# A two-layer hybrid decoder step: the first section behind a norm multiplies rows that are not yet divided by their root mean square

## The reference

```python
def rms_norm(x, g):
    y = x * rsqrt(mean(x * x, axis=-1) + EPS)
    return y * g

for l in (0, 1):
    xn = rms_norm(h, norm_mix_g[l])
    z = xn @ w_in[l]                 # forget, query, value, v, u, ... by columns
    ...                              # gMLP branch, HGRN2 branch, two gates
    h = h + merged @ w_out[l]
    hn = rms_norm(h, norm_ffn_g[l])
    if l == 0:
        h = h + (silu(hn @ w_gate) * (hn @ w_up)) @ w_down
    else:
        h = h + moe_swiglu(hn, ...)  # top 2 of 8 experts
y = rms_norm(h, final_norm_g)
```

## Time and profile before

| | |
|---|---|
| median of three runs | 1613.34 us |
| profiled execution | 1615.19 us, of which span 1613.3 us |
| TensorE busy | 1578.9 us, 98% |
| VectorE, ScalarE busy | 1169.3 us, 1007.7 us |
| up to 800 us (both mixers, dense channel mixer) | 125 to 147 GB/s moved |
| from 800 us (experts) | 354 GB/s moved |

### The profile page before, as it was taken

How to read it: one execution, slowest core, us unless ns; L and a number is a source line. 1 busy time by engine, 2 the same in 40 slices (tenths; PEclk the granted TensorE clock), 3 DMA queues, 4 the chain that set the end, 5 groups by cost and what they waited for, 6 DMA issues and landing times.

```text
span 1613.3 us, 25617 instructions
## 1 busy us (share of the span) xinstructions
PE 1578.9 (98%) x8952; PEld 1403.4 (87%) x8953; DVE 1169.3 (72%) x1493; ACT 1007.7 (62%) x1192; POOL 98.7 (6%) x104
## 2 busy tenths in 40 slices
PE   8999999999999999999999999999999999999997
PEld 8889999999999978999988888888888888888785
DVE  6567437644444577734758989898998989899797
ACT  5663324434333576333467888888888887887785
POOL 3001110000000000021010001000100100000000
PEclk9999989999999999999999999999999999999999
DMA  7434444455445433433469999999999999999995
GB/s 240 132 106 135 149 136 127 130 145 154 140 144 159 126 114 109 131 138 131 127 203 363 375 374 375 368 379 362 381 378 377 376 371 382 364 372 369 373 366 200
DMA packets 223103, 398.57 MB, mean 247 GB/s; under 512 B 12369, under 2 KB 103553, under 8 KB 223025
## 3 DMA queue, kind: packets, MB, share of 16 engines
q1 hardware_dynamic: 215920, 372.84, 66.3%
q0 software_dynamic: 6752, 24.02, 4.9%
q10 hardware_dynamic: 352, 0.66, 0.1%
HBM read 383.84 MB, written 13.63 MB: 246 GB/s over the span
## 4 chain that ended last, share of the span: by engine, by line
PE 83%; DVE 6%; ACT 5%; issue 3%; DMA 3%; ACTq 0%; DVEq 0%; POOL 0%; SPq 0%; POOLq 0%
PE bank L1562 10%; PE bank L1564 10%; PE bank L1563 10%; PE bank L1907 10%; PE bank L1909 9%; PE bank L1908 9%; PE bank L1896 4%; PE bank L1898 4%; PE bank L1897 4%; ACT weights_high L709 2%; DMA weights_raw<-in_moe_w_up 1%; PE bank L1748 1%; PE bank L1874 1%; PE bank L1798 1%; PE bank L1793 1%
## 5 line engine op out<-in xcount | busy, mean ns | idle before, releaser
L1430 DVE TENSOR_TENSOR weights_low<-weights_raw,weights_high 128x1024 fp32r<-128x1024 f32 x522 | 619.4, 1222 | 77.9 <-ACT weights_high L940 68.4
L940 ACT ACTIVATE weights_high<-weights_raw 128x1024 fp32r<-128x1024 f32 x522 | 548.6, 1060 | 138.5 <-DMA weights_raw<-in_moe_w_up 46.0
L1026 DVE TENSOR_TENSOR weights_low<-weights_raw,weights_high 128x1024 fp32r<-128x1024 f32 (+1 forms) x186 | 224.6, 1213 | 294.7 <-ACT weights_high L709 294.5
L709 ACT ACTIVATE weights_high<-weights_raw 128x1024 fp32r<-128x1024 f32 (+1 forms) x186 | 193.6, 1045 | 246.8 <-PE bank L1564 236.2
L1562 PE MATMUL bank<-moving_high,weights_high 128*128 128x320 f32 x944 | 301.0, 319 | 0.7 <-DVE moving_low L1100 0.7
L1563 PE MATMUL bank<-moving_low,weights_high 128*128 128x320 f32 x944 | 296.9, 315 | 0.0
L1564 PE MATMUL bank<-moving_high,weights_low 128*128 128x320 f32 x944 | 296.9, 314 | 0.0
L1907 PE MATMUL bank<-weights_high,expert_in_high 128*128 128x512 f32 (+1 forms) x768 | 290.1, 378 | 2.6 <-DVE weights_low L1430 2.2
L1909 PE MATMUL bank<-weights_high,expert_in_low 128*128 128x512 f32 (+1 forms) x768 | 286.2, 373 | 0.0
L1908 PE MATMUL bank<-weights_low,expert_in_high 128*128 128x512 f32 (+1 forms) x768 | 286.1, 373 | 0.0
L1562 PEld LDWEIGHTS bank<-moving_high,weights_high 128*128 128x128 f32 x944 | 182.5, 193 | 4.0 <-DVE moving_low L1100 1.6
(11 more groups left out here) (327 smaller groups left out, 1837.6 us busy)
## 6 DMA issues: line engine op xcount, KB each, us to landing
weights_raw<-in_moe_w_gate SPq DMA_DIRECT2D x176, 512.0 KB, 5.5
weights_raw<-in_moe_w_up SPq DMA_DIRECT2D x176, 512.0 KB, 5.7
weights_raw<-in_moe_w_down SPq DMA_DIRECT2D x176, 512.0 KB, 5.3
weights_raw<-in_w_in SPq DMA_DIRECT2D x80, 512.0 KB, 3.6
weights_raw<-in_dense_w_gate SPq DMA_DIRECT2D x22, 512.0 KB, 3.7
weights_raw<-in_dense_w_up SPq DMA_DIRECT2D x22, 512.0 KB, 3.7
weights_raw<-in_w_out SPq DMA_DIRECT2D x16, 512.0 KB, 3.4
weights_raw<-in_dense_w_down SPq DMA_DIRECT2D x16, 512.0 KB, 3.4
```

Source lines behind the costliest of these rows:

```text
L709: fn(whi[:, p % RING, 0:n], raw[:, p % RING, 0:n], ACT.Copy).then_inc(high_done, 1)
L940: fn(whi[:, p % RING, 0:n], raw[:, p % RING, 0:n], ACT.Copy).then_inc(high_done, 1)
L1430: v.tensor_tensor(wlo[:, p % RING, 0:n], raw[:, p % RING, 0:n], whi[:, p % RING, 0:n].bitcast(F), ALU.subtract).then_inc(low_done, 1)
```

## The change

Behind each of the three norms the first section (forget 0, gate 0, forget 0 of layer 1) no longer waits for the norm. VectorE multiplies each group of the residual by the gain alone (`scale_residual`) as soon as the group is final, ScalarE makes the high part, VectorE the low part, and `products_as_scaled` multiplies them. TensorE takes the mean square behind the fifth of eight groups and spreads the inverse root behind the seventh. The second section uses the fully normed rows as before. ScalarE copies the first section's two output tiles out, and VectorE multiplies them by the inverse root (`first_outputs_divided`); for the gate the SiLU follows behind that. The identity turns inside the norms are gone (the 38 at the start stay).

```diff
+        def scale_residual(n, j):
+            col = (P_FFN if n % 2 else P_MIX) + KD * (n // 2) + j
+            v.tensor_scalar(xn[:, j, :], h[:, j, :], prm[:, col:col + 1], None, ALU.mult).then_inc(scaled_ready, 1)
+
+        def scaled_low_part(n, j):
+            high, low = scaled_operands(n)
+            dve.wait_ge(scaled_high, KD * n + j + 1)
+            v.tensor_tensor(low[:, j, :], xn[:, j, :], high[:, j, :].bitcast(F), ALU.subtract).then_inc(scaled_low, 1)
+
+        def first_outputs_divided(out, L, sec):
+            for j in (0, 1):
+                dve.wait_ge(act_emptied, tile[(L, sec, j)][3])
+                v.tensor_tensor(out[:, j, :], out[:, j, :], bank[4][:, 0:T], ALU.mult).then_inc(scaled_out, 1)
...
-        split_low(0, 0)
         dve.wait_ge(prm_ready, 1)
...
-        norm(0, after_inverse=lambda: split_low(0, 1))
+        scale_residual(0, 0)
+        split_low(0, 0)
+        for j in range(1, KD + 1):
+            if j < KD:
+                scale_residual(0, j)
+            if j == KD // 2:
+                split_low(0, 1)
+            scaled_low_part(0, j - 1)
+        norm(0, after_inverse=lambda: split_low(1, 0), midway=lambda: split_low(1, 1))
         v.tensor_tensor(lbt[:, 0], ...).then_inc(lb_ready, 1)
-        for c in range(1, AHEAD):
+        for c in range(2, AHEAD):
             split_low(c, 0)
             split_low(c, 1)
...
+        def products_as_scaled(L, sec, c, tiles, n):
...
+                    pe.wait_ge(scaled_low, KD * n + k + 1)
...
+                    if k == STAT_AFTER:
+                        mean_square(n)
+                    if k == SPREAD_AFTER:
+                        spread_root(n)
...
                 elif i == 0:
+                    products_as_scaled(L, sec, c, (2 * part, 2 * part + 1), ns)
+                elif i == 1:
                     products_as_normed(L, sec, c, (2 * part, 2 * part + 1), ns)
```

More of the change, by code:

```diff
@@ L242, in hybrid_trunk_program @@
     xt = later("x_rows", [128, NT, D], F, z_at)
+    rh = later("scaled_high", [128, KD, T], R, region)
+    rl = later("scaled_low", [128, KD, T], R, region + 2 * W5)
     fh = later("hidden_high", [128, KF, T], R, region)
@@ L326, in hybrid_trunk_program @@
     spread_psum = sem("inverse_rms_spread")
+    scaled_ready = sem("scaled_residual_ready")
+    scaled_high = sem("scaled_high_ready")
+    scaled_low = sem("scaled_low_ready")
+    scaled_out = sem("first_outputs_divided")
+    scaled_silu = sem("first_gates_silu_ready")
     xn_ready = sem("normed_ready")
@@ L723, in square, with scaled_high_part, norm @@
             fn(sq[:, j % 2, :], bank[j % 4][:, 0:T] if n == 0 and j % 2 else h[:, j, :], ACT.Square).then_inc(squared, 1)
-        def norm(n, parts=True, after_root=None):
+        def scaled_high_part(n, j):
+            act.wait_ge(scaled_ready, KD * n + j + 1)
+            fn(scaled_operands(n)[0][:, j, :], xn[:, j, :], ACT.Copy).then_inc(scaled_high, 1)
+        def norm(n, parts=True, after_root=None, midway=None):
             act.wait_ge(stat_psum, n + 1)
@@ L733, in norm @@
                 for j in range(KD):
+                    if midway and j == KD // 2:
+                        midway()
+                    if n % 2 == 0:
+                        act.wait_ge(pe_mark, mark_after[2 * base(n // 2) + j // (KD // 2)])
                     act.wait_ge(xn_ready, KD * n + j + 1)
@@ L754, in _ @@
         split_high(0, 0)
-        norm(0, after_root=lambda: split_high(0, 1))
-        for c in range(1, AHEAD):
+        for j in range(KD):
+            if j == KD // 2:
+                split_high(0, 1)
+            scaled_high_part(0, j)
+        norm(0, after_root=lambda: split_high(1, 0), midway=lambda: split_high(1, 1))
+        for c in range(2, AHEAD):
             split_high(c, 0)
@@ L829, in _ @@
                         normed_rows(0)
+                    if L < LAST:
+                        for j in (2 * part, 2 * part + 1):
+                            scaled_high_part(2 * L + 1, j)
                     for j in (2 * part, 2 * part + 1):
@@ L896, in _ @@
                         for j in (0, 1):
-                            empties(L, sec, 2 * part + j, sg[:, j, :], ACT.Silu)
+                            empties(L, sec, 2 * part + j, sg[:, j, :], ACT.Silu if part else ACT.Copy)
+                    if sec == "up" and part == 0:
+                        act.wait_ge(scaled_out, 4 * L + 4)
+                        for j in (0, 1):
+                            fn(sg[:, j, :], sg[:, j, :], ACT.Silu).then_inc(scaled_silu, 1)
                     if sec == "down" and part == 3:
@@ L900, in _ @@
                     if sec == "down" and part % 3 == 2:
+                        for j in (0, 1):
+                            scaled_high_part(2 * L + 2, 2 * (part // 3) + j)
                         for j in (0, 1):
@@ L1037, in add_square, with norm @@
                 v.tensor_tensor(ssum[:], ssum[:], sq[:, j % 2, :], ALU.add).then_inc(summed, 1)
-        def norm(n, parts=True, after_inverse=None):
+        def scale_residual(n, j):
[6 more added lines that the diff above has]
+        def first_outputs_divided(out, L, sec):
+            for j in (0, 1):
+                dve.wait_ge(act_emptied, tile[(L, sec, j)][3])
+                v.tensor_tensor(out[:, j, :], out[:, j, :], bank[4][:, 0:T], ALU.mult).then_inc(scaled_out, 1)
+        def norm(n, parts=True, after_inverse=None, midway=None):
             col = (P_FFN if n % 2 else P_MIX) + KD * (n // 2)
@@ L1311, in _ @@
                     c = first_chunk[(L, "gate")] + i
+                    if i == 1:
+                        first_outputs_divided(sg, L, "gate")
                     split_low(c + AHEAD, 0)
@@ L1316, in _ @@
                             dve.wait_ge(act_emptied, tile[(L, "gate", 2 * part + j)][3])
+                            if part == 0:
+                                dve.wait_ge(scaled_silu, 2 * (L // 2) + j + 1)
                             if part:
@@ L1320, in _ @@
                     if sec == "down" and part % 3 == 2:
-                        for j in (0, 1):
-                            add_residual(L, sec, 2 * (part // 3) + j)
+                        for j in (2 * (part // 3), 2 * (part // 3) + 1):
+                            add_residual(L, sec, j)
+                            dve.wait_ge(dve_emptied, tile[(L, sec, j)][3])
+                            scale_residual(2 * L + 2, j)
+                        for j in (2 * (part // 3), 2 * (part // 3) + 1):
+                            scaled_low_part(2 * L + 2, j)
                         for j in (0, 1):
@@ L1627, in mean_square @@
             ins.then_inc(spread_psum, 1)
-            turn_identity(KEEP[n][2])
+        def products_as_scaled(L, sec, c, tiles, n):
+            _, kt, cols = chunks[c]
+            high, low = scaled_operands(n)
+            for half in range(2):
+                p = 2 * c + half
+                pe.wait_ge(low_done, p + 1)
+                if half == 0:
+                    for t in tiles:
+                        opens(L, sec, t)
+                for q in range(kt // 2):
+                    k = half * (kt // 2) + q
+                    pe.wait_ge(scaled_low, KD * n + k + 1)
+                    for m, t in enumerate(tiles):
+                        w = slice(q * cols + 128 * m, q * cols + 128 * m + 128)
+                        b = bank[tile[(L, sec, t)][0]]
+                        mm(b[:, 0:T], whi[:, p % RING, w], high[:, k, :], start=k == 0, stop=False)
+                        mm(b[:, 0:T], whi[:, p % RING, w], low[:, k, :], start=False, stop=False)
+                        ins = mm(b[:, 0:T], wlo[:, p % RING, w], high[:, k, :], start=False, stop=k == KD - 1)
+                        if k == KD - 1 or k == kt // 2 - 1 and m == len(tiles) - 1:
+                            ins.then_inc(pe_mark, 1)
+                    if k == STAT_AFTER:
+                        mean_square(n)
+                    if k == SPREAD_AFTER:
+                        spread_root(n)
         pe.wait_ge(first_ready, 3)
```

30 lines of the change are left out of this document (17 added, 13 removed).

## The result

The changed kernel takes 1627.36 us (median of 12 runs, 1618.81 to 1633.99); the kernel before, run beside it, 1612.74 (12 runs, 1610.07 to 1616.53). The ratio is 1.0086, 95% interval 1.0071 to 1.0101: 14 us slower. The forecast was 1623.3 us, range 1617.5 to 1629.5.

A forecast was written before the change was run, and what follows sets the result against it. VectorE's and ScalarE's list ending in `spatial_transposed` was taken to bound the first mixer, TensorE most else. 9.8 + 2.4 - 3.6 - 1.0 + 2.4 = +10.0 us on 1613.34 gave 1623.3 us, range 1617.5 to 1629.5.

The forecast's parts named there:

- rival Two: Norm 0: TensorE stays at 1.2 GHz through the whole scaled section, 4.1 us more, 1627.4 us; 12 in 100.
- norm 0: TensorE leaves the second section: First mixer: matmuls behind the second section, waiting for `spatial_transposed`, begin at 47.4 instead of 37.66, 9.8 us lost.
- clock behind that pause, up to norm 1's place: After norm 0's pause, towards VectorE's last w_out addition to the residual: 1.2 GHz work costs 2.4 us.
- norm 1: No list behind it: scaled products begin at 293.48, second section at 302.84 instead of 306.43, 3.6 us won.
- norm 2: Second section ends 4.1 us earlier, but TensorE stands 3.1 us for `spatial_transposed`; 1.0 us won.
- clock behind that pause, and the rest of the mixer: Behind norm 2's new 3.1 us pause: TensorE falls to 1.2 GHz, 2.4 us lost, ends 0 and 3.3.
- expert part: Behind the dense part, where expert weights stream: no term in the sum, 0 us.
- The list from VectorE's first norm instruction on: Norm 0, VectorE's and ScalarE's work up to the end of `spatial_transposed`: 18.6 us, from 28.8 to 47.4.
- that case: Norm 0: clock level rises at 22.6 again, 16 products cost 0.296 and 14 cost 0.148; norm begins at 28.3.
- One: Rival: the clock does not fall in the new pauses; +5.2 us, 1618.5 us; 12 in 100.
- Three: Rival: `spatial_transposed` is done before TensorE ends the second section at norms 0 and 2; -5.7, 1607.6 us; 4 in 100.
- Four: Rival: the dense part's loss is hidden in the expert part, where weights stream; 1613.3 us; 6 in 100.

The follow-up runs named there:

- norm0_only: Changed kernel with only norm 0's first section scaled before the division, norms 1 and 2 as in the kernel before; 1630.37 us, ratio 1.0095.
- warm: Changed kernel plus 28 identity turns on TensorE ahead of norm 0's first scaled product; 1628.97 us, ratio 1.0078.
- late_spread: Changed kernel with the matmuls on `spatial_transposed` and VectorE's masking of them moved from the second to the fifth mixer section; 1617.42 us, ratio 1.0012.
- bounds_late: Changed kernel with the `spatial_transposed` matmuls and masking moved to the fifth section and the lower-bound terms to layer 0's third section; 1613.96 us, ratio 0.9995.
- turns: Changed kernel plus 70 and 24 identity turns on TensorE in the pauses at norms 0 and 2, ahead of its wait; 1624.22 us, ratio 1.0058.
- bounds_moved: Changed kernel with the lower-bound terms, used only in layer 1, moved from norm 0's list to layer 0's third section; 1623.77 us, ratio 1.0051.
- none: Kernel before's instruction order, nothing scaled, built from the variants' code with more semaphores and some added VectorE waits; 1619.16 us, ratio 1.0032.
- norm2_only: Changed kernel with only norm 2's first section scaled before the division, norms 0 and 1 as in the kernel before; 1618.81 us, ratio 1.0036.

## Why the prediction was right

The side, the mechanism and the place were right, and the time fell in the range, 4 us above the forecast. That it is rival Two's 1627.4 us to the digit is chance; that rival's mechanism did not occur. By the steps of the sum:

| step | predicted us | measured us |
|---|---|---|
| norm 0: TensorE leaves the second section | +9.8 (47.4) | +9.6 (47.29) |
| clock behind that pause, up to norm 1's place | +2.4 | +3.1 |
| norm 1 | -3.6 | -3.9 |
| norm 2 | -1.0 | -1.3 |
| clock behind that pause, and the rest of the mixer | +2.4 | +4.6 |
| expert part | 0 | +1.9 |
| sum | +10.0 | +14.0 |

The second row's measure is the 12.7 us at norm 1's place less 9.6; the third is 306.44 to 315.24 less these 12.7; the fourth is the 7.6 us at 559.86 less the 8.9 at norm 2's begin; the fifth 12.2 less 7.6; the sixth 14.1 less 12.2. The sum is 0.1 under the span's 14.1 by rounding and by what lies between norms 1 and 2.

**Norm 0.** The list from VectorE's first norm instruction on was worked out as 18.6 us, from 28.8 to 47.4. Measured it was 18.8, from 28.48 to 47.29. Counted from the spread, which begins 1.0 us before that instruction, it took 19.81, 19.82 and 19.81 us in three runs with different begins (the changed kernel, norm0_only, warm) and 16.7 with 3.1 us of work taken out. That the pace in the first mixer is set by the end of a list and not by the first product is shown. The Trainium skill (TensorE: Matmul & The Clock Gate, Architectural detail) says that VectorE's and ScalarE's queues are strictly first in, first out. These runs agree: `spatial_transposed`, which needs only transposes that TensorE had made by 30, stood behind terms that layer 1 alone uses until 46.56, and came 3.1 us earlier against the spread when these were gone.

The prediction was too narrow in one thing. It took the wait for `spatial_transposed` as the loss. late_spread took that wait away and at norm 0 won back only 3.7 of 12.7 us, since ScalarE's copy, begun 2.9 us ahead in the same lists (43.69 against 46.56 in the changed kernel), was the next to be late. Only with the terms moved as well did the loss go (bounds_late).

One small figure was off. The prediction gave a product at 0.50 twice the 0.148 us, 0.296; in the changed kernel such products begin 0.267 us apart. But the level rose at 23.7 and not at 22.6, and the two nearly cancel: the norm began at 28.48, against 28.3 for that case and 28.8 as taken.

**The clock behind the pauses** is the term that was mis-sized: 2.4 us each, where the slow pace from 47.3 to 54.4 and from 560 to 566.4 cost 3.2 and 2.9 (the begin of the third section's ninth group of products against the kernel before, less the shift at the matmuls ahead), and some 1.7 us more went to other slow stretches in layer 1's mixer. Counted as one less the granted clock over 1 us rows, what was lost between norm 2 and the experts is 8.5 us before and 13.6 in the changed kernel, 3.4 of it at the new pause. The 2.4 was read from rows too far apart. Behind the first pause of the earlier trace rows the level did not fall at 120.19 but at 121.6, so that pause cost 1.7 by the same count and the second 3.4:

```profile
120.00:121.00 1.00, 0.81 (x6) 0.70 (x6) 1.00 (x2) 0.00 (x0) 0.24 (x1) 1.00 0.00 0
121.00:122.00 1.00, 1.00 (x6) 0.93 (x7) 1.00 (x2) 0.00 (x0) 0.30 (x1) 0.79 0.19 45
```

turns shows the whole: the expert part begins 6.9 us earlier when the pauses are filled. One value for each pause was the weak form of this term. In bounds_moved the same pause at norm 2 cost nothing.

**Norm 1 and norm 2** came as worked out within 0.3 us, and the copies behind norm 1 held nothing up: TensorE's one wait between 293 and 340 was 0.2 us. **The expert part** was put at nothing; it took 1.9 us more, and none, with 2.3 us more, shows that this much comes without any change of order. Of the rivals, One is out for the changed kernel (the clock fell twice; in bounds_moved it did not fall at norm 2), Two as well (0.50 ended by 24, in the section), Three and Four too (the wait ended at 47, and the expert part hid none of the 12.2 us).

The 0.2% that the prediction took as the smallest difference that can be told was too small for this kernel: none stands at 0.32%. The changed kernel's 0.86% is above that, and 12.2 us of its 14 are seen in the trace ahead of the experts.

## What to carry to other kernels

Where several engines work off written lists, starting the consumer earlier wins only if the producers' lists end earlier; look for the last item that the consumer needs, and first for work in front of it that nobody needs yet. Here the same idea lost 10 us or more where such a list stood behind it (norm 0) and won 3.9 where none did (norm 1), so it is worth applying by place. Read small changes at a fixed point of the trace, and run the unchanged program once through the same build before trusting 0.3%.

## What the runs showed of the hardware

The clock's answer to a pause differed from run to run. Losses are counted here as one less the granted clock over 1 us rows. Two pauses of 1.9 us (ends at 34.2 and 40.2) were followed by 1.00 in bounds_late, and the first of them (end at 34.6) by a loss of 1.7 us in late_spread. The same pause of 2.9 us at norm 2 was followed by no loss in bounds_moved, by 1.7 us in norm2_only, and by 3.4 in the changed kernel and in warm. In the 8.1 us pause 1.00 was granted until 44, some 5 us into it. The sum of such losses between norm 2 and the experts went from 6.8 to 13.6 us over these kernels, though TensorE's waits there differed by little more than that one pause; that alone moves a run of the dense part by several us.

The same order of instructions, with some waits added, gave 1.0032 [1.0013, 1.0051] in another program. The traced executions of the two took 1616.14 and 1615.19 us: ahead of the experts none was 1.3 us quicker (820.8 against 822.1), from there on 2.3 us slower, where the weights stream with the DMA engines' share near 1.0. That execution is 3.0 us under none's median, so no trace shows where most of the 0.3% lies.
